# Out projection in a pass for each token half, first gate and up products at its end, last pair finished in place

## The reference, cut to what matters

```python
xn   = rms_norm(h, g_pre_mix)
q, k, v, gate_b, gate_c, conv_in = split(xn @ w_in)
attn = stick_breaking_attention(q, k, v)              # 8 heads x 128
conv = gate_b * causal_conv3(gate_c * conv_in)        # 8 groups x 128
mix  = concat(group_rms_norm(attn), group_rms_norm(conv))
h    = h + rms_norm(mix @ w_out, g_post_mix)
xf   = rms_norm(h, g_pre_ffn)
ff   = silu(xf @ w_gate) * (xf @ w_up)                # 5632 wide
h    = h + rms_norm(ff @ w_down, g_post_ffn)
```

## Time and profile before

| what | value |
|---|---|
| median of 3 runs | 2453.63 us (2452.96 to 2456.07) |
| profiled execution, own time | 2450.74 us |
| its span, first to last instruction | 2449.0 us, 42232 instructions |
| mean granted TensorE clock | 0.987 |
| PE busy | 2374.5 us (97%), 18280 matmuls |
| DVE busy | 1541.6 us (63%) |
| ACT busy | 1011.0 us (41%) |
| POOL busy | 81.9 us (3%) |
| chain that ended last | PE 90%, DVE 5%, DMA 2%, ACT 2%, issue 1% |
| DMA | 327.93 MB, mean 134 GB/s |

### The profile page before, as it was taken

The page is one execution under the profiler, slowest core; times in us unless marked ns, Lnnn a source line. Parts: engine busy times, 40 slices in busy tenths (PEclk is TensorE's granted clock), DMA queues, the critical chain, the costliest instruction groups (busy, mean ns, idle before and its releaser), DMA issues.

```text
span 2449.0 us, 42232 instructions
## 1 busy us (share of the span) xinstructions
PE 2374.5 (97%) x18280; PEld 2334.6 (95%) x18280; DVE 1541.6 (63%) x1778; ACT 1011.0 (41%) x1245; POOL 81.9 (3%) x143
## 2 busy tenths in 40 slices
PE   8999999999999996699999999999999899999998
PEld 7999999999999995699999999999999899999998
DVE  5323333343434225877777777777777688888887
ACT  6345444432333223444444444444444333333346
POOL 0000000000002110000000000000000000000002
PEclk9999999999999998799999999999999999999999
DMA  7222322222324331234445444444445666645562
GB/s 234 84 75 70 97 77 79 74 87 87 87 81 146 99 104 73 75 130 133 154 135 168 136 154 149 132 155 134 154 134 168 246 210 231 231 143 156 183 204 87
DMA packets 325916, 327.93 MB, mean 134 GB/s; under 512 B 8508, under 2 KB 282324, under 8 KB 325604
## 3 DMA queue, kind: packets, MB, share of 16 engines
q1 hardware_dynamic: 299264, 275.57, 35.9%
q10 hardware_dynamic: 26468, 49.67, 5.5%
HBM read 264.20 MB, written 61.00 MB: 133 GB/s over the span
## 4 chain that ended last, share of the span: by engine, by line
PE 90%; DVE 5%; DMA 2%; ACT 2%; issue 1%; SPq 0%; POOL 0%; ACTq 0%; DVEq 0%; POOLq 0%
PE ps L955 37%; PE ps L438 30%; PE ps L1012 17%; PE ps L722 4%; DMA ff_lo_scr<-hid_lo 2%; PE ps L666 1%; DVE xs L1800 1%; DVE t_lo L1778 1%; DVE misc L1804 0%; DVE panel L1792 0%; DVE wide L1768 0%; DVE misc L1772 0%; ACT xs L1350 0%; DMA panel<-in_w_down_dram 0%; DMA misc<-in_x_sample_dram 0%
## 5 line engine op out<-in xcount | busy, mean ns | idle before, releaser
L955 PE MATMUL ps<-xs,t_hi 128*128 128x272 f32 x4928 | 940.6, 291 | 33.0 <-DVE xs L1800 19.1
L955 PEld LDWEIGHTS ps<-xs,t_hi 128*128 128x128 f32 x4928 | 781.1, 190 | 34.6 <-issue 32.2
L955 PE MATMUL ps<-xs,t_lo 128*128 128x272 f32 x2464 | 716.8, 291 | 0.0
L1778 DVE TENSOR_TENSOR t_lo<-panel,t_hi 128x1024 fp32r<-128x1024 f32 (+1 forms) x405 | 485.5, 1199 | 228.3 <-ACT t_hi L1343 225.3
L1343 ACT CAST t_hi<-panel 128x1024 fp32r<-128x1024 f32 (+1 forms) x405 | 413.4, 1021 | 455.1 <-PE ps L1012 241.9
L1012 PE MATMUL ps<-xd,t_hi 128*128 128x272 f32 x2464 | 470.4, 290 | 14.3 <-DVE y_left L1949 8.2
L955 PEld LDWEIGHTS ps<-xs,t_lo 128*128 128x128 f32 x2464 | 467.3, 190 | 0.0
L438 PE MATMUL ps<-act_hi,w_hi 128*128 128x272 f32 (+1 forms) x2048 | 435.4, 294 | 3.1 <-DVE act_lo L1615 1.9
L438 PE MATMUL ps<-act_lo,w_hi 128*128 128x272 f32 (+1 forms) x2048 | 426.9, 290 | 0.0
L438 PE MATMUL ps<-act_hi,w_lo 128*128 128x272 f32 (+1 forms) x2048 | 426.5, 289 | 0.0
L1012 PEld LDWEIGHTS ps<-xd,t_hi 128*128 128x128 f32 x2464 | 390.7, 190 | 15.5 <-issue 15.4
(11 more groups left out here) (183 smaller groups left out, 1728.4 us busy)
## 6 DMA issues: line engine op xcount, KB each, us to landing
w_raw<-in_w_in_dram SPq DMA_DIRECT2D x96, 512.0 KB, 3.8
panel<-in_w_up_dram SPq DMA_DIRECT2D x44, 1024.0 KB, 5.6
panel<-in_w_gate_dram SPq DMA_DIRECT2D x43, 1024.0 KB, 5.1
panel<-in_w_down_dram SPq DMA_DIRECT2D x32, 1024.0 KB, 5.9
ff_hi_scr<-hid_hi SPq DMA_DIRECT2D x22, 952.0 KB, 4.5
ff_lo_scr<-hid_lo SPq DMA_DIRECT2D x22, 952.0 KB, 7.4
w_raw<-in_w_out_dram SPq DMA_DIRECT2D x32, 512.0 KB, 3.9
xd<-ff_hi_scr ACTq DMA_DIRECT2D x28, 544.0 KB, 8.0
```

The source lines that it names most:

```text
L955: mm = nc.tensor.matmul(out, w[:, k, :], xs[:, x, part, k, :], start=begins and k == 0 and w is hi and part == 0, stop=k == KH - 1 and w i ...
L1778: V.tensor_tensor(tile_of(t_lo, i), raw_tile(i), tile_of(t_hi, i).bitcast(F32), ALU.subtract)\
```

## The change

Four edits.

- **The out projection runs once for each half of the tokens.** A chunk e = 16 t + n is now output block n for token half t: 272 tokens, 48 matmuls in one PSUM bank of four, two weight tiles of 24 matmuls each. So `w_out` is loaded, rounded and split twice: 64 tiles in place of 32, and four more tiles behind them. Half 0's row factor, residual sum, squares, next factor, normalising and the operands A11 and A12 are made while TensorE multiplies half 1. The squares of half 0 are folded by DVE in four levels to one block, and TensorE waits for them (`h2_summed`) after chunk 24. h is stored from ACT's queue.
- **Four products are drawn ahead** (PRE = 4): B11 and B21 of steps 0 and 1 run from the four additional tiles between the end of the out projection and the rest of step 0, among the sums of half 1's squares. The ring's numbering (`ring`, `step_of`, `products_by`) skips these four tiles.
- **The sums S1 and S2** are written to buffers of their own, and the operands of `xs` lie in another order in memory, with `xd`'s buffers (`XD_AT`) to match.
- **The last pair is finished in place and earlier.** `times_gate(43)` writes into the gate's own buffer and no longer waits for the store of pair 20; `times_gate_rest(43)` waits for it and copies the block over. The sums are formed in down's step d = 0, the rounding is in d = 0 and the split in d = 1, each earlier than before, and SP's store of the last pair stands ahead of the load of panel (46, 1), not behind it.

```diff
-    OUT_T = 2 * KC
+    OUT_T = 4 * KC + 4
...
+        PRE = 4
+        def products_by(step, q):
+            if step == 1 and q <= B21:
+                return q + 3
+            return 7 * step + q + (3 if step == 0 and q > B21 else 1)
+        def ring(step, q):
+            return 7 * step + q - (2 if step == 0 else PRE)
+        def step_of(i):
+            return (0, i + 2) if i < 5 else divmod(i + PRE, 7)
... (SP)
-            for q in range(2, KC // 2):
+            for q in range(2, KC):
                 load_out(q)
+            for k in range(PRE):
+                load((4, KC, T_OUT), k, gate_up[k // 2][:, TK * (k % 2):TK * (k % 2 + 1), 0:P])
...
-            for g in range(KC // 2):
-                sp.wait_ge(h2_made, g + 1)
-                sp.dma_start(h_scr[:, 2 * g:2 * g + 2, LATE], resid[:, 2 * g:2 * g + 2, LATE])                  .then_inc(h2_stored, 16)
...
+                if step == LAST + 3:
+                    store_hidden(FF // 2 - 1)
                 load_panel(step, 1)
-                if step > 3 and step % 2 == 0 and step // 2 - 2 < FF // 2:
+                if step > 3 and step % 2 == 0 and step // 2 - 2 < FF // 2 - 1:
                     store_hidden(step // 2 - 2)
... (TensorE)
+            for e in range(2, 2 * KC):
+                if e >= 4:
+                    pe.wait_ge(out_copied, e - 3)
+                if e == KC:
+                    pe.wait_ge(mix_late, 4)
+                for half in range(2):
+                    pe.wait_ge(lo_ready, T_OUT + 2 * e + half + 1)
+                    out_part(e, half, list(range(TK)))
+                if e == KC:
+                    out_sums(0)
+                if e == KC + 8:
+                    pe.wait_ge(h2_summed, 4)
+                    nc.tensor.matmul(ps[:, 5, 0:TH], neg1[:, :], h2_sq[0][:, 0, :], start=True, stop=True)\
+                        .then_inc(ms_ready, 1)
+            out_sums(1)
...
+            pe.wait_ge(ms_log, 3)
+            pre_product(0)
+            pre_product(1)
+            h2_sums(0)
+            pre_product(2)
+            for g in range(1, 4):
+                h2_sums(g)
+            pre_product(3)
... (ACT)
+            for e in range(2 * KC):
+                t, n, q = e // KC, e % KC, e // 2
+                for half in range(2):
+                    ahead = 2 * e + half + LEAD
+                    if 2 * e + half >= 2 and ahead < OUT_T:
+                        round_weights((4, ahead // 4, T_OUT), ahead % 4)
+                if e in (3, 5, 7, 9):
+                    mix_high_late((e - 3) // 2)
+                if n == KC - 1:
+                    load_log_table(1)
+                act.wait_ge(chunk_done, CH_OUT + e + 1)
...
+                A(squares[n % 2][:, t * TH:(t + 1) * TH], ps[:, n % 4, 0:TH], ACT.Square).then_inc(sq_made, 1)
+                if e == KC:
+                    make_rstd(1)
+                if e in (KC + 4, KC + 6):
+                    for g in range(2):
+                        square_stream(0, e - KC - 4 + g)
+                if e == KC + 9:
+                    make_rstd(2)
...
+            make_rstd(3)
+            for g in range(4):
+                square_stream(1, g)
+            load_log_table(2)
+            tile_high(ring(0, T2))
+            make_rstd(4)
+            act.wait_ge(product_done, PRE)
+            x_high(A22, x_block(KH, KH, 1), x_normed, 8)
+            x_high(S2, s2_raw[:, :, :], s_made, 2)
... (DVE)
+            for e in range(2 * KC):
+                t, n = e // KC, e % KC
...  (rest_of_weights for the same two tiles as ACT)
+                dve.wait_ge(sq_made, e + 1)
+                V.tensor_scalar(wide_c[:, n, tokens_of(t)], ps[:, n % 4, 0:TH], column(n + C_POSTMIX), None, ALU.mult)\
+                    .then_inc(out_copied, 1)
+                if e in (KC + 1, KC + 2):
+                    for g in range(2):
+                        scale_mix(0, 2 * (e - KC - 1) + g)
+                if e in (KC + 3, KC + 5):
+                    for g in range(2):
+                        add_mix(0, e - KC - 3 + g)
+                if e == KC + 7:
+                    fold_squares(0)
+                if e == KC + 8:
+                    for level in range(1, 4):
+                        fold_squares(level)
+                if e == KC + 10:
+                    dve.wait_ge(rstd_ready, 3)
+                    dve.wait_ge(h2_stored, 16 * 4)
+                    normalize(0, 0, 4)
+                    normalize(0, 4, 4)
...
+            for g in range(-1, 4):
+                if g + 1 < 4:
+                    scale_mix(1, g + 1)
+                if g >= 0:
+                    add_mix(1, g)
             combine(0, T1)
             combine(0, T2)
             combine(0, T3)
+            tile_rest(ring(0, T2))
+            dve.wait_ge(rstd_ready, 5)
...
+            V.tensor_tensor(s1_raw[:, :, :], a21, a22, ALU.add).then_inc(s_made, 1)
+            dve.wait_ge(product_done, PRE)
+            dve.wait_ge(s_made, 1)
+            V.tensor_tensor(s2_raw[:, :, :], s1_raw[:, :, :], a11, ALU.subtract).then_inc(s_made, 1)
             x_rest(A22, 4, a22)
             V.tensor_tensor(a21, a11, a21, ALU.subtract).then_inc(s_made, 1)
+            x_rest(S2, 5, s2_raw[:, :, :])
+            V.tensor_tensor(a12, a12, s2_raw[:, :, :], ALU.subtract).then_inc(s_made, 1)
... (DVE, times_gate and times_gate_rest)
-                if step > 1:
+                if 1 < step < LAST:
                     dve.wait_ge(hid_stored, 32 * (step // 2))
+                out = quarter(gate if step == LAST else hid, 0, 1)
+                V.tensor_tensor(out, step_bank(step, "a"), quarter(gate, 0, 1), ALU.mult).then_inc(c12_up, 1)
...
                 dve.wait_ge(c21_made, step + 1)
+                if step == LAST:
+                    dve.wait_ge(hid_stored, 32 * (step // 2))
+                    dve.wait_ge(c12_up, FF // 2)
+                    V.tensor_copy(quarter(hid, 0, 1), quarter(gate, 0, 1))
... (DVE, down's loop: order after the change)
                 tile_rest(ring(step, T3))
                 combine(step, T4)
                 if d == 0:
                     times_gate(LAST)
+                take_down(d, B11)
+                tile_rest(ring(step, T1))
+                take_down(d, B21)
+                tile_rest(ring(step, T4))
                 if d == 1:
+                    hidden_rest(FF // 2 - 1)
+                take_down(d, T2)
+                tile_rest(ring(step, B22))
                 if d == 0:
                     times_gate_rest(LAST)
+                    hidden_sums(FF // 2 - 1)
                 take_down(d, T3)
+                if d == 0:
+                    more_hidden_sums(FF // 2 - 1)
```

More of the change, by code:

```diff
@@ L929, in _ @@
-            pe.wait_ge(chunk_copied, CH_OUT)
[L930 to L944, removed]
@@ new lines, in out_sums @@
+            def out_sums(t):
+                for part, (x, added_up) in enumerate(((buf_g[:, tokens_of(t)], (sq_added, (KC - 1) * (t + 1))),
+                                                      (squares[(KC - 1) % 2][:, t * TH:(t + 1) * TH],
+                                                       (sq_made, KC * (t + 1))))):
+                    pe.wait_ge(*added_up)
+                    mm = nc.tensor.matmul(ps[:, 4 + 2 * t, 0:TH], neg1[:, :], x, start=part == 0, stop=part == 1)
+                mm.then_inc(ms_ready, 1)
@@ new lines, in _, with pre_product @@
+            out_sums(1)
+            def pre_product(k):
+                step, q = k // 2, k % 2
+                pe.wait_ge(lo_ready, T_OUT + 4 * KC + k + 1)
+                pe.wait_ge(xs_lo, 3 if q else 2)
+                pe.wait_ge(out_copied, 2 * KC)
+                hi, lo = (w[:, k, :].rearrange("p (k n) -> p k n", k=TK) for w in (w_hi, w_lo))
+                for c in range(KH):
+                    for w, part in ((hi, 0), (hi, 1), (lo, 0)):
+                        mm = nc.tensor.matmul(step_bank(step, "ac"[q]), w[:, c, :], xs[q][:, part, c, :],
+                                              start=c == 0 and w is hi and part == 0, stop=c == KH - 1 and w is lo,
+                                              skip_group_check=True)
+                mm.then_inc(product_done, 1)
@@ new lines, in h2_sums @@
+            def h2_sums(g):
+                pe.wait_ge(h2_squared, 4 + g + 1)
+                for c in range(4 * g, 4 * g + 4):
+                    mm = nc.tensor.matmul(ps[:, 7, 0:TH], neg1[:, :], h2_sq[1][:, c, :], start=c == 0, stop=c == KC - 1)
+                if g == 3:
+                    mm.then_inc(ms_ready, 1)
+            pe.wait_ge(ms_log, 3)
[5 more added lines that the diff above has]
+                h2_sums(g)
@@ L963, in _ @@
                 for q in range(7):
-                    i = 7 * step + q
+                    if step < 2 and q <= B21:
+                        continue
+                    i = ring(step, q)
                     pe.wait_ge(tile_lo, i + 1)
@@ L1323, in _, with x_block @@
[L1323 to L1332 removed]
+            def x_block(c0, n, t):
```

(14 more changed lines are left out.)

367 lines of the change are left out of this document (185 added, 182 removed).

## The result

The changed kernel takes 2461.05 us (median of 10 runs, 2459.45 to 2466.9), the kernel before beside it 2453.64 (10 runs): ratio 1.0033, interval 1.0024 to 1.0043. It is slower by 7.4 us, and the forecast of 2438 missed by 23.

A forecast was written before the change was run, and what follows sets the result against it. TensorE, busy 97%, was taken as the bound, so only its waits could pay: 1.6 us from the out projection to the first full step plus 14 at the start of down, 15.6 less, median 2438, range 2426 to 2450.

The forecast's parts named there:

- The read-back: Out projection: h's load between tiles 7 and 8 makes tile 8 land 17.2 us after issue, TensorE idle 9 to 10.
- the wait at chunk 24: Out projection: TensorE waits for DVE's last folds of half 0's squares, idle 9 to 10 us, then 2.5 lost.
- Rival 3: Out projection: slower raw buffer turn, deciding from 7.0 us; at 7.15 it costs 22 us, giving 2460; chance 0.08.
- (c): Out projection: two raw buffers set the pace, a turn of 6.30 us against 6.05 wanted; h stores add 2 (0 to 5).
- Z: End of the last out projection matmul: 934.57 us before, forecast at 970, with break-even there at 971.6.
- The second look at (c): Out projection: splits starting before GpSimd's square sums cost nothing; if each paid 0.35 us, 22 turns would cost 7.7.
- from Z to the factor: After the last out matmul: half-width square, Ln and exp give the row factor in about 3.2 us, 4.6 before.
- the products drawn ahead: After the out projection: four products, 12.1 us, lie beside the factor's chain, hidden; two belong to step 1, 6.05 less left.
- Z+55.4: Step 0: start of product B22, 55.4 us after the last out matmul, against 87.2 before.
- The start of down: Start of down: two TensorE waits shrink, saving 9.5 us at the first and 4.6 at the second, 14 (9 to 16).
- rival 2: Start of down: late store and panel behind it keep the second wait, 8 of 14 us not had, 2446; chance 0.17.
- rival 1: Out projection: weights keep pace, chunk 24 waits only 3.3 us, the pass ends 13.5 earlier: 2424.5; chance 0.12.

The follow-up runs named there:

- experiment 4: The changed kernel without the four stores of h for token half 0 and without the waits for them: 2456.47 us, ratio 1.0013.
- Experiment 1: Two kernels: the one before with only the new ending of the last pair, 2447.50 us; the changed kernel with the old ending, 2468.86 us.
- experiment 5: The kernel before with the last pair's new ending, but panel (46, 1) loaded ahead of the pair's store: 2442.88 us, ratio 0.9955.
- experiment 2: The changed kernel with a third raw weight buffer from tile 8 of the out projection on: 2434.51 us, ratio 0.9924.
- experiment 6: The changed kernel with four raw buffers, tiles 8 and 9 loaded before the read-back, sum after chunk 25: 2426.56 us; also panel before store: 2424.72.

## Why the prediction was wrong

**Right: the place, the list of waits, and which term would decide.** The read-back on its 16.97 us, TensorE idle 9.64 behind it (forecast 9 to 10), casts of tiles two apart as their loads land, the fold that ends the wait at chunk 24 (6.8 us, after 3.4 for tile 49; forecast 9 to 10 in one), the seven chunks at full rate behind it (932.15 to 976.2, 44.0 with the slow product; forecast 44.9): each is in the trace. Rival 3 named the turn of the raw buffer as the deciding number, 7.0 as its threshold and 2460 as its time at 7.15. The turn is 6.86, under that threshold. That the median of 2461.05 falls on the rival's time is luck: two further losses, told below, came on top.

**The step that failed first: (c), the turn of 6.30 us.** ACT and DVE take their 1.05 and 1.24; all the excess is in the landings. Z comes at 976.2 instead of 970. Tile 8 was 4.3 us earlier than forecast (split at 776.8, not 781.1, since SP came to the read-back at 757.13, not 761.6), and the 22 turns took 12.4 more than 22 x 6.30, of which (c) had 2. The 22 landings sum to 99.2 us, against 22 x 3.95 = 86.9 at the usual value. Of the 12.3, four loads of 5.42 to 5.55 make 6.1, the two beside the h stores (5.99 and 7.28) 5.4, and the one after them (4.63) 0.7. The stores were a term of (c), sized at 2 with a bound of 5; experiment 4 puts them at 3 to 4 us. The slow loads were not in the sum. The earlier trace rows had its sign, the one landing of 4.4, and the prediction took the median of a distribution whose long values add up in a ring: 3.9 is what the load takes most often, 4.5 its mean here.

The second look at (c) held. The 55 splits from 780 to 976 us take 1.21 to 1.23 each, while GpSimd's half-width sums take 0.77 where no split runs beside them and about 1.5 where they start behind one. That the one that starts second pays, as the Trainium skill has it (SBUF — State Buffer, "Who interferes with whom"), agrees with the trace. Of the 7.7 us at risk nothing was lost.

**The second step: from Z to the factor, 3.2 us.** The prediction let the half-width square start as soon as the last chunk stood. ACT makes it in its written order, behind tiles 65 and 66, and those hang on the same two buffers; 5.27 us of TensorE's wait is this. The price of the ring was thus charged once, up to Z, and fell due again behind it: Z to the scale 10.7 us, 7.5 more than forecast. Further on the second factor took 8.1 from the last add instead of 5.8. ACT stood 2.3 us there for TensorE's sums of squares: the last three groups of them take 5.51 us and stand behind product 2 of those drawn ahead (3.02 us), at a granted clock of 1.00. By an estimate from these rows (1.84 a group, the squares ready at 994.1, 996.5 and 997.7) they would have ended 2.2 us earlier without that product, so the products drawn ahead, forecast as hidden, were not wholly hidden. The normalising took 6.7 instead of 5.6. In sum B22 begins 11.1 us later than Z+55.4, so with the 6.2 of Z it is 17.3 for the transition. Experiment 1 measured about the same by subtraction: 15.6 lost against 1.6 to be gained is 17.2.

**The third step: the start of down, 14 us.** The first 9.5, the wait of 8.2 and its half clock, came nearly as forecast: 8.9 by the count of matmuls. The second part, 4.6 to be gained, lost 2.5. The panel behind the stores was given 11 to 14 us to land and takes 15.0 to 15.3, so the wait is 5.0 and not 1.5, and the ending gave 5.8. That is rival 2's mechanism, at its price of 8 us. It was held for an alternative to the forecast and was on top of everything else. Of these 8 us the place of the panel behind the stores makes 4.6 to 5.5 (experiment 5); where the rest went was not traced.

**What each part costs, as the runs have it.** With the loads kept ahead (experiment 2) the same change is 18.8 us faster than before: more than the 15.6 forecast with the ring at 6.30. The prediction's rival 1, weights that keep pace, 2424.5, is near the 2426.56 of experiment 6, though that has further edits in it.

## What to carry to other kernels

When a change halves the work that each loaded tile feeds, compare the new interval between tiles with the whole turn of the buffer (landing, rounding, split, release), and use the mean of all landings of that load with its slow ones, not the median: once the turn is above the interval, every slow landing is added to the time. A margin of minus 4% (6.30 against 6.05) is no small term; it puts the stream in the chain, and everything that later waits for it, in the engines' written orders, is late again. Ask first whether a third buffer fits: here it lay unused, and turned a loss of 7 us into a gain of 19.

## What the runs showed of the hardware

In the changed kernel a load of 512 KB lands in 3.8 to 4.0 us as a rule, but in 5.42 to 5.55 for four of the 22 on the ring, each with a 16 KB instruction packet in its window; three others with such a packet landed in 3.99 to 4.02. Four stores of 544 KB on another queue had two loads beside them that took 5.99 and 7.28 us; without the stores they took 4.24 and 5.98. A panel of 1 MB behind 1.9 MB of stores on the same queue takes 15.0 to 15.3 us, and 9.7 when it is issued ahead of them (experiment 5); in the kernel before it took 12.8.

TensorE's granted clock near the end differs between executions of nearly the same code: 1.00 before, 0.51 (the lower of the two levels, 1.2 GHz) over 10 us in the changed kernel's profiled execution, each time after a stretch in which TensorE was busy 7.8 of 10 us. In that execution it goes with 4.9 us, two thirds of the change's effect. It has to be taken out before two profiles are compared.
